# Seven norms of a residual sum: strip sums moved between the tiles of the product they follow

## The reference

```python
# block one, LayerNorm after each residual sum
x = layer_norm(DEEPNORM_ALPHA * x + gate1 * t, ln1_g[l], ln1_b[l])
h = layer_norm(x) * (1.0 + scale2) + shift2
f = channel_mixer(h, w_up[l], ffn_dw_w[l], ffn_dw_b[l], w_down[l])
x = layer_norm(DEEPNORM_ALPHA * x + gate2 * f, ln2_g[l], ln2_b[l])
...
# block two, RMS norm
x = ffn_sub(x, mod_lat[0:3], norm1_w[l], ffn1_w1[l], ffn1_w2[l])
h_lat = modulate(rmsnorm(x, norm2_w[l]), mod_lat[3], mod_lat[4])
...
x = x + mod_lat[5] * lat_mix
x = ffn_sub(x, mod_lat[6:9], norm3_w[l], ffn2_w1[l], ffn2_w2[l])
return rmsnorm(x, final_norm_w)
...
# block three, RMS norm
h = h + hybrid_mixer(rmsnorm_3(h, attn_norm_g[l]), ...)
h = h + swiglu_3(rmsnorm_3(h, ffn_norm_g[l]), w_gate[l], w_up[l], w_down[l])
h = rmsnorm_3(h, final_norm_g)
```

## Time and profile before

| | |
|---|---|
| time, median of 3 runs (lowest, highest) | 3765.47 us (3764.24, 3767.09) |
| the profiled execution: its own time, its span | 3765.76 us, 3763.9 us |
| PE, share of the span busy | 90% |
| DVE, ACT, POOL, shares | 46%, 30%, 26% |
| mean granted TensorE clock | 0.935 of full speed |
| share of time of the weight DMAs (queue q1) on 16 engines | 25.3% |

### The profile page before, as it was taken

The page is one execution under the profiler, slowest core; times in us unless marked ns, Lnnn a source line. Parts: engine busy times, 40 slices in busy tenths (PEclk is TensorE's granted clock), DMA queues, the critical chain, the costliest instruction groups (busy, mean ns, idle before and its releaser), DMA issues. The chain is left out here.

```text
span 3763.9 us, 41980 instructions
## 1 busy us (share of the span) xinstructions
PE 3388.4 (90%) x16962; PEld 2677.9 (71%) x16962; DVE 1717.5 (46%) x2689; ACT 1133.5 (30%) x1777; POOL 977.1 (26%) x414
## 2 busy tenths in 40 slices
PE   4999977998999799999999678889999787889998
PEld 3887744876888588888888566257888563568887
DVE  5995556755331322345510896542211467632211
ACT  2222323324443422122131113323222322543322
POOL 0001310442444222322332002013444221024443
PEclk8999988998999899999999778889999888899999
DMA  4232421542323222343421001012233110012332
GB/s 175 94 101 79 151 65 46 184 162 91 97 98 94 74 79 85 117 135 127 142 68 56 1 1 51 1 47 82 96 110 94 56 52 26 1 57 86 99 96 84
DMA packets 91197, 315.98 MB, mean 84 GB/s; under 512 B 10742, under 2 KB 12534, under 8 KB 90234
## 3 DMA queue, kind: packets, MB, share of 16 engines
q1 hardware_dynamic: 88060, 303.69, 25.3%
q10 hardware_dynamic: 2944, 9.60, 0.7%
HBM read 311.16 MB, written 2.10 MB: 83 GB/s over the span
## 5 line engine op out<-in xcount | busy, mean ns | idle before, releaser
L245 POOL TENSOR_TENSOR terms<-streams,terms 128x1024 fp32r<-128x1024 f32 (+2 forms) x410 | 976.9, 2383 | 2764.4 <-ACT terms L233 2764.4
L455 PE MATMUL bank<-terms,terms 128*128 128x512 f32 (+2 forms) x4016 | 1506.8, 375 | 61.0 <-DVE terms L699 17.8
L456 PE MATMUL bank<-terms,terms 128*128 128x512 f32 (+2 forms) x4016 | 1498.6, 373 | 0.0
L457 PE MATMUL bank<-terms,terms 128*128 128x512 f32 (+2 forms) x4016 | 1495.8, 372 | 0.0
L233 ACT ACTIVATE terms<-streams 128x1024 fp32r<-128x1024 f32 (+1 forms) x462 | 475.6, 1030 | 1842.2 <-PE bank L457 1664.5
L455 PEld LDWEIGHTS bank<-terms,terms 128*128 128x128 f32 x4016 | 763.8, 190 | 216.7 <-issue 65.7
L457 PEld LDWEIGHTS bank<-terms,terms 128*128 128x128 f32 x4016 | 764.5, 190 | 131.5
L456 PEld LDWEIGHTS bank<-terms,terms 128*128 128x128 f32 x4016 | 765.6, 191 | 126.2
L1556 DVE TENSOR_TENSOR stage<-stage,bank 128x256 f32<-128x256 f32 (+1 forms) x88 | 54.6, 622 | 597.7 <-ACT stage L1546 597.7
L1063 DVE SCALAR_TENSOR_TENSOR arena<-arena,vec 128x512 f32<-128x512 f32 x240 | 162.6, 748 | 0.2
L1539 DVE TENSOR_TENSOR terms<-stage,terms 128x512 fp32r<-128x512 f32 (+1 forms) x66 | 115.9, 1759 | 0.0
(11 more groups left out here) (310 smaller groups left out, 3038.9 us busy)
## 6 DMA issues: line engine op xcount, KB each, us to landing
streams<-in_ffn_w SPq DMA_DIRECT2D x104, 512.0 KB, 3.5
streams<-in_w_mod SPq DMA_DIRECT2D x72, 512.0 KB, 3.6
streams<-in_w_up SPq DMA_DIRECT2D x44, 512.0 KB, 3.5
streams<-in_w_gu SPq DMA_DIRECT2D x44, 512.0 KB, 3.6
streams<-in_w_ada SPq DMA_DIRECT2D x32, 512.0 KB, 3.5
streams<-in_w_down SPq DMA_DIRECT2D x32, 512.0 KB, 3.5
streams<-in_w_v SPq DMA_DIRECT2D x24, 512.0 KB, 3.8
streams<-in_ffn_w SPq DMA_DIRECT2D x24, 384.0 KB, 3.4
```

Source lines behind the costliest of these rows:

```text
L245: gp.tensor_tensor(self.low(m), self.raw(n), self.high(m), ALU.subtract).then_inc(self.low_made.sem, 1)
L455: pe.matmul(out, high[:, at], x_high, start=kk == start, stop=False)
L456: pe.matmul(out, high[:, at], x_low, start=False, stop=False)
L457: mm = pe.matmul(out, low[:, at], x_high, start=False, stop=kk == kts - 1)
```

## The change

A new pass `Following` holds a product and the norm behind it. On PE it puts the strip sums of tile i - 1 behind the matmuls of tile i, and the sums of the last tile right behind those. On ACT it puts the square of tile i behind the `make_high`s of step i. For a LayerNorm only the sums of the tiles themselves move; its squares stay where they were. Squares and sums that are moved count on two signals of their own, `squared` and `summed`. All seven norms named above are treated so. The bank of the sums is then in use during the product: at `ffn1_w2`, whose tiles take two banks each, the product gets six banks and the sums one of the other two. The squares of the meta tokens' norm move to another buffer.

```diff
-        self.counts = {k.pe_done: self.means + nt, k.act_done: nt + nt * self.act_each,
-                       k.dve_done: self.centred + nt, k.parted: nt if parts else 0,
...
+        own = streamed and not center
+        self.square_told, self.sum_told = (k.squared, k.summed) if own else (k.act_done, k.pe_done)
+        self.mean_told = k.summed if streamed else k.pe_done
+        self.squares_in, self.means_in = 0 if own else nt, 0 if streamed else self.means
...
     def tensor(self, pe):
         if self.center:
-            self.means_of(pe)
+            if not self.streamed:
+                self.means_of(pe)
             self.means_widened(pe)
-        self.sums(pe)
+        if self.center or not self.streamed:
+            self.sums(pe)
         self.widened(pe)
...
+    def mean_of(self, pe, j):
+        if j == 0:
+            self.bank_there(pe, self.mean_bank)
+        if self.after:
+            self.after(pe, j)
+        mm = self.by_strips(pe, self.mean_bank, self.src(j), j == 0, j == self.nt - 1)
+        if j == self.nt - 1:
+            mm.then_inc(self.mean_told.sem, 1)
...
+    def sum_of(self, pe, j):
+        if j == 0:
+            self.bank_there(pe, self.sum_bank)
+        pe.wait_ge(*self.square_told(j + 1))
+        self.by_strips(pe, self.sum_bank, self.squared(j), j == 0, j == self.nt - 1).then_inc(self.sum_told.sem, 1)
...
+class Following(Pass):
+    def __init__(self, dense, norm):
+        self.dense, self.norm, self.steps, self.counts = dense, norm, dense.steps, dense.counts
+        self.of = norm.mean_of if norm.center else norm.sum_of
...
+    def tensor_step(self, pe, i):
+        self.dense.tensor_step(pe, i)
+        if i:
+            self.of(pe, i - 1)
+        if i == self.steps - 1:
+            self.of(pe, i)
...
+    def scalar_step(self, act, i):
+        self.dense.scalar_step(act, i)
+        if not self.norm.center:
+            self.norm.square_of(act, i)
...
-    return [Vectors(k), gated, LaterGains(k), mixed_in, Reload(k), mixed, ln1, second, LoadContext(k), up], down
+    return [Vectors(k), gated, LaterGains(k), mixed_in, Reload(k), Following(mixed, ln1), ln1, second, LoadContext(k), up], down
...
+        k.bank_set, k.bank_turn = range(6 + 2 * (1 - n)), 0
...
+    last = passes.pop()
+    k.bank_set, k.bank_turn = [6, 7], 0
+    lat2 = modulated(24, 2, 1, lambda eng, j: last.evicted(eng, j, 1), B2_WHOLE, True)
+    k.bank_set, k.bank_turn = range(8), 0
+    passes.append(Following(last, lat2))
     passes.append(SecondGains(k, 72, 24, 72, ((2, 0), (3, 1), (4, 0)), ((7, 64, 0),)))
-    passes.append(modulated(24, 2, 1, lambda eng, j: last.evicted(eng, j, 1), B2_WHOLE))
+    passes.append(lat2)
...
-    return [halves, mixed, middle, up, down, final]
+    return [halves, Following(mixed, middle), middle, up, Following(down, final), final]
```

More of the change, by code:

```diff
@@ L614, in means_of @@
     def means_of(self, pe):
[L615 to L621, removed]
+        for j in range(self.nt):
+            self.mean_of(pe, j)
+    def mean_of(self, pe, j):
[6 more added lines that the diff above has]
+            mm.then_inc(self.mean_told.sem, 1)
     def means_widened(self, pe):
@@ L628, in sums @@
     def sums(self, pe):
[L629 to L633, removed]
+        for j in range(self.nt):
+            self.sum_of(pe, j)
+    def sum_of(self, pe, j):
[3 more added lines that the diff above has]
+        self.by_strips(pe, self.sum_bank, self.squared(j), j == 0, j == self.nt - 1).then_inc(self.sum_told.sem, 1)
     def widened(self, pe):
@@ L642, in scalar @@
             self.averages(act)
-        self.squares(act)
+        if self.center or not self.streamed:
+            self.squares(act)
         self.root(act)
@@ L655, in squares, with square_of @@
     def squares(self, act):
-        k = self.k
         for j in range(self.nt):
[L658 to L665, removed]
+            self.square_of(act, j)
+    def square_of(self, act, j):
+        if self.center:
+            act.wait_ge(*self.k.dve_done(j + 1))
+        elif self.after:
+            self.after(act, j)
+        if j >= self.slots:
+            act.wait_ge(*self.sum_told(self.means_in + j - 2))
+        act.activation(self.squared(j), self.whole(j) if self.center else self.src(j), ACT.Square
+                       ).then_inc(self.square_told.sem, 1)
     def root(self, act):
         k, w = self.k, self.strip
-        act.wait_ge(*k.pe_done(self.means + self.nt))
+        act.wait_ge(*self.sum_told(self.means_in + self.nt))
         if k.widened.base:
@@ L2387, in stream, with modulated @@
         return k.X[:, n, :] if c else k.XC[:, n, :]
-    def modulated(m, at, c, after, whole):
+    def modulated(m, at, c, after, whole, streamed=False):
         n = SEQ if c else CTX
@@ L2442, in block_two @@
     third = Norm(k, lambda j: k.X[:, j, :], lambda j: normed[:, j, :], DT, SEQ, 0, RMS_EPS, False,
-                 lambda j: k.gain[:, 4, j:j + 1], None, lambda j: k.mod2[:, 48 + j:49 + j, 0], h, out.evicted)
+                 lambda j: k.gain[:, 4, j:j + 1], None, lambda j: k.mod2[:, 48 + j:49 + j, 0], h, out.evicted,
+                 streamed=True)
     up = swiglu(k, "ffn2_w1", lambda kk, c: h(kk), LAT_ONLY, hidden, FT, third.ready)
@@ L2446, in block_two @@
                     parted_before(k, FT))
-    meta = Beside(k, down, meta_norm(k), sums=4, squares=2, root=4, inverse=4, widened=5, shifted=5, scaling=5)
     final = Norm(k, lambda j: k.X[:, j, :], lambda j: k.X[:, j, :], DT, SEQ, 0, RMS_EPS, False,
-                 lambda j: k.v("fnorm2", j), after=down.evicted)
-    return [first, heads, halves, out, third, up, LoadMeta(k), meta, final]
+                 lambda j: k.v("fnorm2", j), after=down.evicted, streamed=True)
+    meta = Beside(k, Following(down, final), meta_norm(k), sums=4, squares=2, root=4, inverse=4, widened=5, shifted=5, scaling=5)
+    return [first, heads, halves, Following(out, third), third, up, LoadMeta(k), meta, final]
 T3 = META + SEQ
```

49 lines of the change are left out of this document (35 added, 14 removed).

## The result

The changed kernel takes 3775.6 us (median of 8 runs, 3770.18 to 3777.88) against 3765.31 us of the kernel before beside it (8 runs, 3762.29 to 3776.02). The ratio is 1.0022, 95% interval 1.0013 to 1.0032: slower by some 8 to 10 us. The forecast was 3769.9 us in a range of 3763.5 to 3776; the median lies 5.7 us over the forecast and 0.4 us under the range's upper end. The profiled execution has a span of 3774.1 us and an own time of 3775.88, 10.2 us more than the span before. The mean granted clock is 0.936 (0.935 before), PE is busy 90% of the span, as before.

What follows compares the result with a forecast made beforehand. Inside a product PE was taken as the bound; behind it PE waits and a chain through ACT, PE and DVE sets the time. 20.2 + 0.8 - 16.55 = 4.4 us more gave 3769.9 us, range 3763.5 to 3776.

Steps and rivals of the forecast that it cites:

- the chain: From a product's end to the next product's start, through ACT, PE and DVE: shorter by 16.55 us over the norms.
- what costs nothing on ACT and DVE: Squares between ACT's roundings fit its free time (3.7 us in the shortest tiles), with no table load added: 0.
- Widening: Eight loads behind `w_o3`, `w_out2` or `ffn2_w2` likelier at the lower clock: one case, 0.8 us lost.
- the group: Strip sums between two product tiles on PE: 0.48 us each, 42 x 0.48 = 20.2 us added.
- the way back: On PE, from a group's first weight load to the next product's first matmul: 0.26 us, plus 0.09 behind it.
- The way in: On PE, from a product's last matmul to the first strip weight load: 0.32 us, 0.09 more than a plain step.
- the rival of the drain paid whole: A group between tiles costs 0.65 us, total 3777.0 us; decides from 0.56 us on; chance 0.15.
- the banks: In `ffn1_w2` a tile reuses the bank of three tiles earlier, not four; elsewhere numbers only rotate: no cost.

Runs made afterwards that it cites:

- e5: Kernel before with five RMS norms' squares made early, all sums behind the product (batches of three at `ffn2_w2`), banks as before; 3756.01 us, ratio 0.9975.
- e7: e3 with groups of tiles 1 to 5 taking only 64 of each 128 columns, the other columns' sums left out; one run, 3770.83 us.
- e6: e3 with each moved group made one full-width matmul for a quarter of the tokens, the other sums left out; one run, 3759.52 us.
- e1: The changed kernel, but the first half of `ffn1_w2` goes on in the rotation of the banks; 3771.91 us, ratio 1.0024.
- e2: The kernel before with only the new starting banks of `ffn1_w2` and of the products behind it; 3771.81 us, ratio 1.0014.
- e3: e1 with the two LayerNorms (`w_out`, `w_down`) keeping their sums behind the product, only the five RMS norms moved; 3765.46 us, ratio 1.001.
- e9: The kernel of e4 measured once more; 3759.9 us, ratio 0.9981.
- e4: e3 with sums in batches: tiles 0 to 2 behind tile 3, 3 to 5 behind tile 6, the last two behind tile 7; 3759.03 us, ratio 0.9994.
- e8: The kernel of e5 measured once more; 3757.95 us, ratio 0.997.

## Why the prediction was right or wrong

**Right: the chain.** By norm, forecast and measured: `w_out` 0.6 and 0.61, `w_down` 0 and 0.54, `ffn1_w2` 3.2 and 3.24, `w_out2` 3.65 and 3.86, `ffn2_w2` 3.65 and 3.65, `w_o3` 3.65 and 3.65, `w_down3` 1.8 and 1.80. The sum was 16.55 and came out at 17.35. The reason given, that the root waited for ACT's own squares, is what e5 shows for the RMS norms. In `w_down` the copy stands where it was forecast, behind the Silu; where the half microsecond comes from stays open, and executions with the same norm differ by as much.

**Right: what costs nothing on ACT and DVE.** No rounding slips behind a square: at the ends of tiles in `w_out2` and `w_down3` PE's step is the 0.67 to 0.68 us of a lone group and nowhere more. Both kernels have 33 table loads. Widening: one case of 0.8 us was forecast among three norms; it is there, at `w_out2`, 0.8 us of loads and 0.9 for the next product's start. The term left out the other norms: `w_down3`'s widening lost 0.5 us, and behind `w_down` two widenings won 1.3.

**Mis-sized: the group.** The term was 42 x 0.48 = 20.2 us; it measured 23.6, 0.56 a group (0.585 in the short tiles), less where a group shares its way in with the groups of the context's or the meta tokens' norm. The working took 0.26 us from the earlier trace rows for the way back and argued that "part of it should hide" of the longer array work at 128 columns. e7 shows that none hides: from the first strip load to the next product matmul 0.25 us at 64 columns, 0.36 at 128. The way in, 0.32, was right. 0.56 is the value from which, by the prediction, the rival of the drain paid whole decides; its price of 0.65 was too high, since the 0.21 of the array lies inside the way back and not behind it.

The page TensorEngine Tiling (Array Packing) of the Trainium skill says under Key Properties that a change of tiling mode drains the engine. The traces agree: ahead of strips the first weight load starts 0.31 to 0.32 us behind the start of the last product matmul, in single groups and in batches, and ahead of full-width weights of another matrix it waits 0.01 (e6).

**Wrong: the banks.** The step that failed, a term put at nothing, is "The banks: in `ffn1_w2` a tile now reuses the bank of three tiles earlier, not four, and evictions end some 1.2 us behind each tile; elsewhere numbers only rotate". The distance inside the product was checked, the seam ahead of it was not: a set that starts at 0 again meets the banks of the up projection's last step, which ACT has still to read. That is 2 x 1.85 = 3.7 us, shown by e1 and e2, and it is over half of the miss. The change's own text gives the start of each set of banks; the missing question is who held those banks last.

**The account.** Forecast +4.4 us: -16.55 + 20.2 + 0.8. Measured: -17.35 + 23.6 + 0.9 + 3.7 = +10.8, with +10.2 in the span. The miss is 3.7 of banks and 3.4 of group, less 0.8 of gain. That the time still fell inside the range is in part luck: the prediction reached its upper end of 3776 with groups at 0.62 us, and groups at the measured 0.56 give 3773.3 by its own working; the banks, for which the range had no term, bring the rest. The ratio of 1.0022 lies just outside the 0.2% to which the prediction gave 0.77.

## What to carry to other kernels

When work is moved out of a chain, ask of each engine whether it was the one that the chain waited for: here the place of the squares was worth 16.2 us in the five RMS norms, the place of their sums nothing (shown in four of them), and all moved sums together cost 23.6 us of TensorE time. A small matmul in another tiling mode between full products costs more for its visit (0.35 us here) than for its work (0.21); give such work the time in which the engine waits, or at least one visit for several pieces. Whenever a rotation of buffers is set back to a start, look at who used those buffers last, at every seam and not only inside the loop.

## What the hardware did that was not expected

The same instructions take two different times in block three's attention, by the granted clock. From the last reciprocal ahead of it (3092.53 in the kernel before) to the last matmul of `w_o3`, with the added groups taken off, the profiled executions of the kernel before, the change, e1, e2, e3, e6 and e9 take 281.0 us, those of e4, e5, e7 and e8 291.7 to 291.8. e4 and e9 are one kernel. Busy time by stretch there, e3 and then e5:

```profile
3130.00:3180.00 50.00, 29.69 (x76) 12.77 (x77) 39.60 (x81) 14.76 (x32) 2.34 (x1) 0.80 0.00 0
3180.00:3230.00 50.00, 41.22 (x249) 21.86 (x249) 37.05 (x89) 30.75 (x102) 0.00 (x0) 0.83 0.01 1
```

```profile
3123.00:3173.00 50.00, 29.74 (x73) 12.83 (x74) 38.70 (x80) 14.94 (x31) 2.34 (x1) 0.76 0.00 0
3173.00:3223.00 50.00, 42.31 (x223) 21.41 (x221) 35.85 (x85) 29.15 (x96) 0.00 (x0) 0.76 0.00 1
```

The third column from the end is the granted clock, a mean over the stretch: 0.76 against 0.80 and 0.83, with PE busy about as long (29.69 and 29.74, 41.22 and 42.31 us). In all four long cases, and in none of the others, the stage before (from the first product behind `ffn2_w2`'s norms to that reciprocal) was 3 to 4 us shorter, 144.6 to 145.5 us instead of 148.5 to 148.8. So these four executions were quicker in one partly busy stage and slower in the next, by 7 us in the balance. It shows in the spread: e5 and e8 reach down to 3745.7 and 3746.9 us, 14 under the lowest run of the kernel before beside them, and have medians 8.7 under. It is likely part of the reason why that version gave 9 us of the 14 expected; the runs without a profile do not show their stages.

It is not the only place. e4 has runs at 3758 and at 3780, 22 us apart, and its profiled execution (3778.4 us) lost 8 us in one stretch of block two's mixers, 33.40 us where the same kernel as e9 took 25.45 between the same two instructions. Busy time by stretch, e4 and then e9:

```profile
2427.00:2443.00 16.00, 15.09 (x40) 5.40 (x38) 9.64 (x21) 2.14 (x7) 0.00 (x0) 0.64 0.00 0
```

```profile
2429.40:2445.40 16.00, 15.09 (x56) 5.21 (x54) 11.34 (x25) 5.05 (x14) 0.00 (x0) 1.00 0.00 0
```

PE is busy 15.09 of 16 us in both and starts 40 matmuls at a granted clock of 0.64, 56 at 1.00; from 2431.4 to 2448.5 e4 had the lower of the two levels throughout. From the reciprocal behind `ffn1_w2` to the first eviction of `w_out2`, a stretch that no edit touches, the eleven profiled executions take 620.9 to 632.7 us. What tips an execution one way or the other stays open; no run here moved it on purpose. A difference of a few microseconds between two single executions is therefore read stage by stage and not from the span.
